# Preparing the fourth unit's weights inside the norms, letting the first units of a stage end one by one, adding the first sums on VectorE, and reusing the room of keys and values for attention outputs

## What is computed

```
# first block: (sh1, sc1, g1, ...) = split(silu(c) @ ada_w + ada_b, 9)
y = rmsnorm(h, pre_g) * (1 + sc1) + sh1
y = (silu(y @ w_gate) * (y @ w_up)) @ w_down              # ffn1, width 2816
h = h + 0.5 * g1 * rmsnorm(y, post_g)
y = rmsnorm(h, pre_g) * (1 + sc2) + sh2
h = h + g2 * rmsnorm(token_mix(y), post_g)                # mix: mLSTM and HGRN2 heads
...                                                       # ffn2, like ffn1
# second block: two layers, i = 0 (gla) and i = 1 (differential attention)
h = rmsnorm(x, g) * (1 + scale_t) + shift_t
x = x + gate_t * mixer(h)
h = rmsnorm(x, g) * (1 + scale_c) + shift_c
x = x + gate_c * (square(relu(h @ w1)) @ w2)              # mlp0, mlp1, width 4096
return rmsnorm(x, final_g)
```

## Time and profile before

| | |
|---|---|
| median of 3 runs | 2518.12 us |
| the profiled execution, its own time | 2518.35 us |
| its span | 2516.5 us |
| TensorE busy | 2389.0 us (95%) |
| VectorE, ScalarE, GpSimd busy | 1296.2, 825.8, 239.4 us |
| mean granted TensorE clock | 0.966 |

### The profile page before, as it was taken

The page is one execution under the profiler, slowest core; times in us unless marked ns, Lnnn a source line. Parts: engine busy times, 40 slices in busy tenths (PEclk is TensorE's granted clock), DMA queues, the critical chain, the costliest instruction groups (busy, mean ns, idle before and its releaser), DMA issues.

```text
span 2516.5 us, 26709 instructions
## 1 busy us (share of the span) xinstructions
PE 2389.0 (95%) x10794; PEld 1929.4 (77%) x10794; DVE 1296.2 (52%) x1887; ACT 825.8 (33%) x1225; POOL 239.4 (10%) x188
## 2 busy tenths in 40 slices
PE   8999997999997999999799989999999989899998
PEld 6888885777785788888588868888767767788886
DVE  5654537276247255545434456665356664554343
ACT  3322223223433222223353333223234443333221
POOL 0000005021015000004101100000122111000001
PEclk8999998999998999999899999999999989999999
DMA  7766531311121256541222226664121112243330
GB/s 274 256 205 201 179 118 50 99 44 42 59 59 51 84 175 210 190 138 49 84 92 76 59 85 216 201 207 145 51 99 57 59 43 66 94 142 92 92 101 34
DMA packets 80794, 288.01 MB, mean 114 GB/s; under 512 B 8976, under 2 KB 9104, under 8 KB 80672
## 3 DMA queue, kind: packets, MB, share of 16 engines
q1 hardware_dynamic: 79952, 284.74, 35.4%
q10 hardware_dynamic: 720, 1.57, 0.2%
HBM read 284.18 MB, written 2.10 MB: 114 GB/s over the span
## 4 chain that ended last, share of the span: by engine, by line
PE 82%; DVE 12%; ACT 3%; issue 2%; POOL 1%; DMA 0%; DVEq 0%; SPq 0%; ACTq 0%; POOLq 0%
PE bank L271 21%; PE bank L273 21%; PE bank L272 21%; DVE wlo L1384 2%; PE bank L372 2%; PE bank L342 2%; PE bank L338 2%; PE bank L339 2%; ACT whi L863 1%; PE bank L314 1%; PE bank L316 1%; PE bank L315 1%; PE bank L420 1%; PE bank L366 1%; DVE ylo L1576 1%
## 5 line engine op out<-in xcount | busy, mean ns | idle before, releaser
L1384 DVE TENSOR_TENSOR wlo<-raw,whi 128x1024 fp32r<-128x1024 f32 (+1 forms) x370 | 475.6, 1289 | 493.4 <-ACT whi L863 493.0
L271 PE MATMUL bank<-yhi,whi 128*128 128x512 f32 x1680 | 670.8, 399 | 29.6 <-DVE wlo L1384 21.8
L272 PE MATMUL bank<-ylo,whi 128*128 128x512 f32 x1680 | 660.0, 393 | 0.0
L273 PE MATMUL bank<-yhi,wlo 128*128 128x512 f32 x1680 | 659.7, 393 | 0.0
L863 ACT ACTIVATE whi<-raw 128x1024 fp32r<-128x1024 f32 (+1 forms) x370 | 383.8, 1042 | 423.2 <-PE bank L273 256.9
L271 PEld LDWEIGHTS bank<-yhi,whi 128*128 128x128 f32 x1680 | 318.4, 190 | 118.0 <-issue 47.9
L273 PEld LDWEIGHTS bank<-yhi,wlo 128*128 128x128 f32 x1680 | 318.8, 190 | 67.9
L272 PEld LDWEIGHTS bank<-ylo,whi 128*128 128x128 f32 x1680 | 318.8, 190 | 64.3 <-issue 0.7
L271 PE MATMUL bank<-mlp_ahi,whi 128*128 128x512 f32 x512 | 202.5, 396 | 0.0
L272 PE MATMUL bank<-mlp_alo,whi 128*128 128x512 f32 x512 | 202.5, 396 | 0.0
L273 PE MATMUL bank<-mlp_ahi,wlo 128*128 128x512 f32 x512 | 202.5, 395 | 0.0
(11 more groups left out here) (312 smaller groups left out, 2725.9 us busy)
## 6 DMA issues: line engine op xcount, KB each, us to landing
raw<-in_ada SPq DMA_DIRECT2D x152, 512.0 KB, 4.4
raw<-in_ffn_up SPq DMA_DIRECT2D x88, 512.0 KB, 4.4
raw<-in_mlp_up SPq DMA_DIRECT2D x64, 512.0 KB, 3.7
raw<-in_mlp_dn SPq DMA_DIRECT2D x64, 512.0 KB, 3.7
raw<-in_ffn_dn SPq DMA_DIRECT2D x32, 512.0 KB, 3.7
raw<-in_w_dqkv SPq DMA_DIRECT2D x24, 512.0 KB, 3.7
first<-in_ada SPq DMA_DIRECT2D x16, 512.0 KB, 15.3
raw<-in_ffn_dn SPq DMA_DIRECT2D x16, 384.0 KB, 3.7
```

Source lines behind the costliest of these rows:

```text
L271: e.matmul(out, wh, xh[:, kt, :], start=first, stop=False)
L272: e.matmul(out, wh, xl[:, kt, :], start=False, stop=False)
L273: mm = e.matmul(out, wl, xh[:, kt, :], start=False, stop=last)
L1384: e.tensor_tensor(k.wlo[:, what % NW, 0:width], raw[:, 0:width], k.f(k.whi[:, what % NW, 0:width]), ALU.subtract).then_inc(*sig.up("wlo", ...
```

## The change

It has five parts.

1. **Fourth unit.** In a bridge, both ScalarE and VectorE make `whi`/`wlo` of the next stage's fourth unit before the roots (`prep_to(self.u + NW - 1)`), not in `four` behind the whole norm. Bookkeeping moves with it: a unit that `four` began is later taken from a queue `ahead`, so that each of the four releases a further preparation.
2. **`four`.** The ylo matmuls of a tile stand one tile later. At the last tile each unit does its last two in a row, so the units end one after another. In ffn1, mlp0, diff and mlp1 the second pair follows three tiles behind (`lag` 3).
3. **First sums on VectorE.** At the program's start VectorE adds the eight squares, and TensorE sums one tile instead of eight. One of the eight shift vectors that TensorE made moves (tiles 1 to 4 instead of 0 to 3). In the bridges VectorE adds the `hz` products; GpSimd adds two sums instead of three, and one column sum falls away.
4. **Order in norms.** The bridge loses one `warm`, the first spread stands behind the column sums at once, and VectorE does `post` of tile 0 before the second reciprocal. `prenorm` alternates `scaled` and `low`.
5. **Attention.** The split outputs of heads 0 to 5 go to `dxh`/`dxl`, which lie where keys and values lay, and no longer wait for the last of the 24 units. Their slices stand in more of the steps, the last heads are normed in groups of one, and one `warm(3)` falls away.

```diff
@@ Pe.four
+    def four(self, tags, x, hi, lag=0, before=None):
...
+        for n in range(NT + lag):
+            if before:
+                before(n)
+            for kt, group in ((n, us[0:2]), (n - lag, us[2:4])) if lag else ((n, us),):
                 if not 0 <= kt < NT:
                     continue
+                high(kt, group)
                 for u in group:
+                    for at in range(max(kt - 1, 0), kt if kt < NT - 1 else NT):
+                        low(at, u)
@@ Pe.totals
-        for n in range(NT):
-            self.w.wait_ge(*self.sig.on("sq", st, n))
-            mm = self.column(out, 0, self.k.tm(slot(n)), n == 0, n == NT - 1)
+        self.w.wait_ge(*self.sig.on("dsum", st, 7))
+        self.column(out, 0, self.k.tm(0), True, True).then_inc(*self.sig.up("tot", st))
@@ Pe.bridge
-        w.wait_ge(*sig.on("hzadd", st, 6))
-        self.column(two, 0, k.tm(0), True, False)
...
-        self.warm(1)
         self.root(st, 0)
@@ Pe.diff
+        spread(7)
         self.warm(2)
-        spread(6)
-        spread(7)
-        self.warm(3)
         for n in range(24, 28):
-            for kt in (6, 7):
-                part(n, kt, x)
+            part(n, 7)
+        for n in range(28, 32):
+            for kt in range(8):
+                part(n, kt)
@@ Act.prenorm
+        self.prep_to(self.u + NW - 1)
         if sums[-1] == "h":
@@ Act, Dve: unit and four
     def unit(self, tag):
-        u = self.count(tag)
+        u = self.ahead.popleft() if self.ahead else self.count(tag)
         self.prep_to(u + NW - 1)
         return u
@@ Dve.first_norm
-        for n in range(2):
-            self.ada(1, n)
+        w.wait_ge(*sig.on("sq", "start", 0))
+        for n in range(1, NT):
+            w.wait_ge(*sig.on("sq", "start", n))
+            self.add("start", n, k.tm(n)[:, 0:S])
+        self.ada(1, 0)
+        self.ada(0, 0)
+        self.ada(1, 1)
         self.root("start")
@@ Dve.bridge
         self.need(v_shift)
+        self.prep_to(self.u + NW - 1)
         self.root(st)
...
         post(0)
-        post(1)
+        self.root(st + "h")
         w.wait_ge(*sig.on("post", st, 0))
         e.tensor_tensor(k.h[:, 0, :], k.h[:, 0, :], k.tm(0)[:, 0:S], ALU.add).then_inc(*sig.up("hv", st, 0))
+        post(1)
@@ build_program
+            dxh = sb("dxh", [128, 8, S], f32r, s)
+            dxl = sb("dxl", [128, 4, D], f32r, s)
...
-        k.d_parts += [[], slices[152:155], slices[155:158], slices[158:]]
+        one, two = ([(n + i, kt) for kt in range(7) for i in range(2)] for n in (24, 26))
+        k.d_parts += [slices[152 + 2 * i:154 + 2 * i] + one[i:i + 1] for i in range(4)]
+        k.d_parts += [one[4:8], one[8:12], two[0:4], two[4:8], two[8:10], two[10:12] + one[12:] + two[12:]]
...
-        k.d_normed = {30: (0, 1, 2, 3), 31: (4, 5)}
+        k.d_normed = {24: (0, 1), 25: (2, 3), 29: (4,), 30: (5,), 33: (6,)}
```

More of the change, by code:

```diff
@@ L326, in four, with high @@
         outs = [self.bank("u", u) for u in us]
-        for n in range(NT + (3 if before else 0)):
-            for kt, group in ((n, us[0:2]), (n - 3, us[2:4])) if before else ((n, us),):
+        def high(kt, group):
+            w.wait_ge(*sig.on(hi, *st, kt))
+            c = slice(128 * kt, 128 * kt + 128)
+            for u in group:
+                w.wait_ge(*sig.on("wlo", u))
+                out = outs[u - us[0]]
+                e.matmul(out, k.whi[:, u % NW, c], xh[:, kt, :], start=kt == 0, stop=False)
+                e.matmul(out, k.wlo[:, u % NW, c], xh[:, kt, :], start=False, stop=False)
@@ L350, in shift @@
-        if n >= 3:
+        out = k.banks.at("shift", n % 3) if n > 3 else self.bank("shift", n % 3, hold=True)
+        if n > 3:
             w.wait_ge(*sig.on("mod0", n - 3))
@@ L440, in up @@
                 done = 4
-                self.four([tag] * 4, y, "yhi", self.shift_ahead if st == "ffn1" else None)
+                self.four([tag] * 4, y, "yhi", 0 if st == "ffn2" else 3, self.shift_ahead if st == "ffn1" else None)
             if st == "ffn1" and g == 0:
@@ L698, in diff, with part @@
         y = (k.yhi, k.ylo, "ylo", ("diff",))
[L699 removed]
+        self.four(["dqkv"] * 4, y, "yhi", 3)
         first = self.u - 4
         outs = {}
[L703 removed]
+        def part(n, kt):
             u = first + n
[L706 removed]
+            st = "diff" if n < 24 else "diffx"
+            xh, xl = k.x_in(st, kt)
             if kt == 0:
@@ L825, in program @@
         self.w.wait_ge(k.s_cst, 16)
-        self.warm(4)
-        self.totals("start", lambda n: n)
-        self.shift(0)
+        self.warm(8)
+        self.totals("start")
         self.root("start", 0)
-        for n in (1, 2):
+        for n in SHIFTS[0:2]:
             self.shift(n)
-        self.warm(2)
         self.ffn("ffn1", FFN_GROUPS, True)
@@ L970, in up @@
                 if first:
-                    self.two = self.four([tag] * 4)
-                u = self.two.pop(0) if self.two else self.unit(tag)
+                    self.four([tag] * 4)
+                u = self.unit(tag)
                 buf = k.tm(len(before) % 4)[:, 0:S]
@@ L1470, in prenorm @@
         self.need(v_shift)
-        for n in range(1, 7):
+        for n in range(1, NT):
             scaled(n)
-        low(0)
-        scaled(7)
-        for n in range(1, 8):
-            low(n)
+            low(n - 1)
+        low(7)
     def first_norm(self, g):
@@ L1955, in rotated @@
                 *sig.up("dsinm", n, bank=("turn", n)))
+        for _ in range(4):
+            self.unit("dqkv")
         rotated(0)
@@ L2275, in build_program @@
         k.pc = lambda name, i=0, n=1, p=128: k.par[0:p, offs[name] + i:offs[name] + i + n]
-        k.dgroups = [(g, n, n == size - 1) for g, size in enumerate((4, 2, 2)) for n in range(size)]
+        k.dsizes = (4, 2, 1, 1)
+        k.dgroups = [(g, n, n == size - 1) for g, size in enumerate(k.dsizes) for n in range(size)]
+        six = [(d4(dxh[:, h, :]), dxl[:, :, 128 * h:128 * h + 128]) for h in range(6)]
+        k.x_in = lambda st, kt: six[kt] if st == "diffx" and kt < 6 else (k.yhi[:, kt, :], k.ylo[:, kt, :])
         slices = [(n, kt) for n in range(4, 24) for kt in range(8)]
```

187 lines of the change are left out of this document (93 added, 94 removed).

## The result

The changed kernel takes 2390.45 us (median of four runs, 2388.74 to 2391.95), against 2514.24 us for the kernel before in the same count of runs. The ratio is 0.9508, 95% interval 0.9485 to 0.953. The forecast of faster was right in sign and nearly in size. Of the gain, 18 us came from an edit to which the prediction gave no term.

What follows compares the result with a forecast made beforehand. TensorE was taken as the bound, busy 2389.0 of 2516.5 us; only its idle 127.5 us and low-clock work could move. Terms 53.5 + 11 + 9 + 22 + 16 = 111.5 off 2518.35 gave 2407 us, range 2393 to 2434.

Steps and rivals of the forecast that it cites:

- the first one: Long stretches: TensorE busy all 320.00 us from 80 to 400 us at clock 1.00, so nothing to gain there.
- A: Bridges after ffn1, mix, ffn2: fourth unit's weights made before the roots end stalls and slow restarts; 53.5 us, bounds 35-54.
- D: `four` and units behind it: one-by-one ends and lag remove waits for `wlo` and `ylo`; 22 us, bounds 12 to 24.
- B: Chain from a stage's last unit to the next first matmul, three stages: shorter by 11 us, bounds 5 to 15.
- Rival 3: Bridges of three stages: with one warm fewer, `four` starts at the low clock; 8 us lost, 2415 us; chance 0.06.
- a first reciprocal that starts later behind the column sums: Sign that the forecast is wrong: this reciprocal starts later behind the column sums than before; no size given.
- C: Program's start: squares added on VectorE bring the first scaled tile and last `ylo` earlier; 9 us, bounds 3 and 10.
- E: Attention's tail: the 7.41 us wait, low clock and a warm go, less 4 for new waits; 16 us, bounds 8-20.
- no clock below 0.9: Sign that term E is right: around attention's last 24 units no clock under 0.9 and no wait above 3 us.
- Rival 1: Attention and start give nothing, as the softmax chain and loads pace them; 2432 us; chance 0.20.
- Rivals 2, 4 and 5: `four` hungry or slow, 2464 us (0.12); slower by 0.5% at 1.2 GHz (0.02); bridge's tile or slot not free, 2461 (0.02).

Runs made afterwards that it cites:

- the one line: The kernel before with only the small tile `hs` widened from 48 to 52 words, so activation tiles behind it start 32 bytes later; ratio 0.9927.

## Why the prediction was right and wrong

The step that failed is the first one: "In the long stretches nothing is to be had", with 0.229 us for one matmul. That figure is the mean of two pitches, 0.2267 and 0.2333, over a window that holds units of both kinds. Two windows of 40 us would have shown it. And the edit that joins the two pitches, one line of the diff, stands in no term of the sum: it was put at nothing without a reason. It measured 18.7 us: the last group of matmuls begins at 2506.37 before and at 2487.64 with the one line. In the changed kernel it begins at 2380.93, 125.4 earlier than before. The five terms were to give 111.5; what is left for them is 125.4 - 18.7 = 106.7. Without the 18.7 us the changed kernel would have taken some 2409 us, by my estimate, inside the range.

- **A: 53.5 expected, 54.7 measured.** The stalls and the slow restart are gone, and TensorE has no gap in `four`: 22.0 us for twelve matmuls in each of eight tiles (22 expected), and 1.2 to 1.3 of waiting for the fifth unit. The table's 56.7 includes 2.0 by which that last wait is shorter, which is D's. Undone alone, A costs 50 us. Right.
- **B: 11 expected, 11.8 measured.** The sum is right, its shares are partly luck: 2.1, 6.6 and 3.1 us, where 3 to 4 a stage were expected. The way behind ffn2 was 12.8 us in this profile and 11.1 in three other versions that don't differ there. Rival 3, a start at the low clock for want of a warm, is refuted by the window at 409 and by the warm put back. But the clock does fall inside the bridge, with TensorE busy on one-column matmuls and spreads. Before and after, behind ffn1:

```profile
414.00:417.00 3.00, 3.00 (x9) 1.97 (x10) 0.99 (x6) 0.30 (x1) 0.00 (x0) 0.50 0.00 0
```

```profile
402.40:405.40 3.00, 3.00 (x11) 2.21 (x10) 1.64 (x9) 0.30 (x1) 0.00 (x0) 0.50 0.51 175
```

It is back at 1.00 before `four` begins. The Trainium skill (TensorE: Matmul & The Clock Gate, Why this matters for your kernels) advises to leave no idle gaps between bursts of matmuls. These traces agree that the clock falls behind gaps, but it fell in these places without a long one, too. The sign "a first reciprocal that starts later behind the column sums" did come in ffn1 (4.4 us behind the first column sum, 4.0 before) and cost nothing, as it ends while the column sums still run.
- **C: 9 expected, 7.4 measured.** The first scaled tile comes at 20.97 (21 expected) and the last `ylo` at 51.02 + 0.75 = 51.8 (51 expected). The end of ffn1 gains 11.0 - 3.6 (address) = 7.4. The norm's chain came as forecast, 8.3 us earlier at its end. What was not seen is that TensorE no longer follows it. From 27.41, the first matmul of `four`, to the fifth unit at 60.56 (67.09 before) it waits for nothing, and until 43.77 it works at half the clock, on those matmuls and on the shift vectors:

```profile
20.00:43.00 23.00, 23.00 (x90) 21.07 (x89) 20.45 (x37) 6.45 (x8) 0.00 (x0) 0.50 1.03 409
```

So of the 8.3 us the fifth unit got 6.5.

- **D: 22 expected, 25.0 measured.** `four` in mlp0, attention and mlp1 gives 11.8, the shorter wait behind it in the other three stages 2.0. The rest of mlp0 and mlp1 gives 21.7, of which 10.5 is address: 11.2 remain where the two waits sum to 7.5. The other 3.7 is the clock, 0.57 for the 4 us behind such a wait before:

```profile
1492.00:1496.00 4.00, 4.00 (x12) 3.09 (x12) 3.20 (x4) 2.21 (x4) 0.00 (x0) 0.57 0.78 221
```

The prediction counted that restart in A and E and forgot it here. It came behind short waits, too, in ffn2 behind the one of 1.88 at 843.12 before, and likewise in gla:

```profile
844.00:847.00 3.00, 3.00 (x9) 2.32 (x8) 1.70 (x3) 1.68 (x4) 0.00 (x0) 0.50 0.52 171
```

After, the clock is 1.00 at these places. The rests of ffn2 and gla are 1.6 us shorter each, beyond the address, about what 3.4 us at half the clock cost. Of mechanisms, the lag is the smaller one (5.5 us in all); the ends one by one with the queue did more.

- **E: 16 expected, 5.6 to 8 measured.** Undone in the changed kernel it costs 8. From before to after the rest of attention gains 6.8, of which 1.2 came with the one line on `hs` alone. This is the term that was over-sized. I had priced the wait of 7.41, the clock and the warm in full and took off 4 for new waits. The end of attention has these in its place:

```profile
1943.13 1.13 PE L759 MATMUL bank<-dk,dq 64*128 64x512 f32 x4 [1.35 <-ACT dp L1303]
...
1965.43 0.73 PE L775 MATMUL bank<-daT,dvals 128*128 128x128 f32 x2 [1.57 <-ACT dvals L1265]
...
1975.36 0.51 PE L273 MATMUL bank<-dxh,whi 128*128 128x512 f32 x1 [2.39 <-ACT hs L935]
...
1999.45 0.50 PE L273 MATMUL bank<-dxh,whi 128*128 128x512 f32 x1 [1.73 <-DVE wlo L1388]
```

One long wait became several short ones, and the clock is 0.72 and 0.74 in two windows of 6 us there (1964 and 1976), against the sign "no clock below 0.9". Rival 1 is half right for attention and wrong for the start. The stage's other surprise is the wait of 3.52 at the first softmax step. Before, the units ahead of that step waited 1.88 and 2.12 us for their own weights, and the step found its keys ready.

Rivals 2, 4 and 5 did not come. Without the missing term the sum would have been off by 5 us only, and that is partly luck: E was too high by 8 to 10 and C by 2, A, B and D together too low by 5, and the rests of ffn2 and gla too low by 3. The missing 18.7 made the miss. Left open is why the rest of mix is 1.2 us longer after; with the address line alone it is 318.02, and in other versions of the changed kernel 316.6 to 319.3, so it varies by itself.

## What to carry to other kernels

Before calling a stretch at 100% busy and full clock finished, divide it by its matmuls and compare stretches that move different tiles: a pitch that differs is a cost no list of waits shows. An edit of a tile's width moves all tiles laid out behind it, so read a diff for sizes as well. And where a wait is removed, price the low clock behind it each time, behind short waits as well, and look for what comes late next: it may be TensorE itself at the low clock.

## What the runs showed of the hardware

At a granted clock of 1.00, a matmul of 128x512 in this kernel follows the last one after 0.2267 us (544 cycles at 2.4 GHz) when its weights and its moving tile start at the same byte modulo 128, and after 0.2333 us (560 cycles) when they are 32, 64 or 96 bytes apart, whichever of the two is moved. At distances that are no multiple of 32, 4 bytes gave 0.236, 16 bytes 0.231 and 48 bytes 0.232, and 112 bytes cost nothing (one run). In 40 us at a clock of 1.00 and 100% busy that is 178 matmuls against 173. The cause within the chip was not shown: that the load of the next weights and the reads of the moving tile meet in memory would fit, and is only an idea.

The granted clock fell to 0.50 behind waits as short as 1.88 us (before, 843.12), and in the bridges while TensorE was busy with matmuls of one column (414 to 417 before, 402.4 to 405.4 after). It did not fall behind every such wait: behind the one of 1.88 us at 465.11 it is 1.00 from 465 to 470.
